# Sigmoids and the softmax division as exponentials of minus a logarithm, w_out by half columns first, GLA's last step one group later

## The reference, cut to what matters

```python
u = rmsnorm(h, norm1_w)
aq, ak, av, gq, gk, gv, g_lr, g_r, gate_a, gate_b = split(u @ w_in)
# attention: window 128, a sink logit per head joins the softmax
p = softmax(concat([s, sink]))[..., :-1]
attn_o = p @ v
# GLA: decayed state per head, read per chunk
log_a = log_sigmoid(g_lr @ gla_gate_w2 + gla_gate_b) / 16
gla_o = rmsnorm(gla(gq, gk, gv, log_a), gla_norm_w) * silu(g_r)
merged = sigmoid(gate_a) * attn_o + sigmoid(gate_b) * gla_o
h = h + merged @ w_out
v2 = rmsnorm(h, norm2_w)
h = h + (silu(v2 @ w_gate) * (v2 @ w_up)) @ w_down
out = rmsnorm(h, final_norm_w)
```

## Time and profile before

| | |
|---|---|
| median of 3 runs | 4039.02 us (4012.56, 4039.02, 4191.1) |
| the profiled execution | 3989.18 us, span of its slowest core 3987.6 us |
| spans of the eight cores | 3979.7 to 3987.6 us, granted clock 0.978 to 0.979 |
| TensorE (PE) | 3767.8 us busy, 94% of the span |
| VectorE (DVE) | 1285.7 us, 32% |
| ScalarE (ACT) | 806.1 us, 20% |
| GpSimd (POOL) | 194.3 us, 5% |
| chain that ended last | PE 91%, DVE 4%, DMA 2%, issue 1%, ACT 1% |

### The profile page before, as it was taken

One profiled execution on the slowest core, in us unless ns is written; L12 is line 12 of the kernel. 1 busy time (PEld: TensorE's weight loads), 2 busy tenths in 40 slices (PEclk: granted clock), 3 DMA queues, 4 the chain that ended last, 5 costly groups with the idle time before them and its releaser, 6 DMA issues.

```text
span 3987.6 us, 46220 instructions; the slowest of 8 cores (3979.7 to 3987.6 us)
## 1 busy us (share of the span) xinstructions
PE 3767.8 (94%) x18016; PEld 1700.6 (43%) x18016; DVE 1285.7 (32%) x2070; ACT 806.1 (20%) x1549; POOL 194.3 (5%) x361
## 2 busy tenths in 40 slices
PE   4899999996899999999999999999869999999998
PEld 1444444442344444444454444444324444444443
DVE  1225555556331110011112464646553111110113
ACT  1223232322221110000012232323313000000002
POOL 0000000000000000000000000000000000000000
PEclk9999999998999999999999999999989999999999
DMA  6234343435365555457863434333256555555553
GB/s 152 45 64 69 64 69 64 69 64 119 67 166 119 111 102 85 71 109 146 161 126 64 69 64 69 64 69 64 43 137 153 106 109 119 119 106 93 134 103 111
DMA packets 81416, 382.75 MB, mean 96 GB/s; under 512 B 9264, under 2 KB 10416, under 8 KB 44592
## 3 DMA queue, kind: packets, MB, share of 16 engines
q0 software_dynamic: 36432, 260.19, 39.2%
q1 hardware_dynamic: 44768, 119.59, 9.2%
HBM read 594.84 MB, written 44.04 MB: 160 GB/s over the span
## 4 chain that ended last, share of the span: by engine, by line
PE 91%; DVE 4%; DMA 2%; issue 1%; ACT 1%; POOL 0%; DVEq 0%; SPq 0%; ACTq 0%; POOLq 0%
PE ps L331 89%; DMA px_231<-xT 1%; DVE a_t_93 L378 1%; PE ps L339 1%; PE ps L619 1%; DMA h_0_96<-x 1%; DVE xnT_102 L375 1%; POOL st L399 0%; DVE xn_100 L375 0%; DVE mT L369 0%; ACT g_Sb L355 0%; DVE xn_101 L375 0%; DVE g_U L375 0%; DVE a_t_94 L364 0%; DVE a_t_93 L364 0%
## 5 line engine op out<-in xcount | busy, mean ns | idle before, releaser
L378 DVE RECIPROCAL a_t_93<-a_t_93 128x512 f32<-128x512 f32 x64 | 214.5, 3352 | 6.6
L355 ACT ACTIVATE sg_212<-ps 128x512 bf16<-128x512 f32 x88 | 52.5, 597 | 541.5 <-PE ps L331 541.5
L355 ACT ACTIVATE sg_213<-ps 128x512 bf16<-128x512 f32 x88 | 52.6, 598 | 527.8 <-PE ps L331 527.8
L331 PE MATMUL ps<-v2T_163,wu_67 128*128 128x512 bf16 x576 | 136.1, 379 | 0.0
L331 PE MATMUL ps<-v2T_108,wu_68 128*128 128x512 bf16 x576 | 136.1, 379 | 0.0
L331 PE MATMUL ps<-v2T_108,wu_65 128*128 128x512 bf16 x576 | 136.1, 379 | 0.0
L331 PE MATMUL ps<-v2T_108,wu_66 128*128 128x512 bf16 x576 | 136.1, 379 | 0.0
L331 PE MATMUL ps<-v2T_163,wu_69 128*128 128x512 bf16 x576 | 136.1, 379 | 0.0
L331 PE MATMUL ps<-v2T_108,wu_69 128*128 128x512 bf16 x576 | 136.1, 379 | 0.0
L331 PE MATMUL ps<-v2T_163,wu_66 128*128 128x512 bf16 x576 | 136.1, 379 | 0.0
L331 PE MATMUL ps<-v2T_163,wu_65 128*128 128x512 bf16 x576 | 136.1, 379 | 0.0
(11 more groups left out here) (1319 smaller groups left out, 6541.1 us busy)
## 6 DMA issues: line engine op xcount, KB each, us to landing
wu_66<-wmix POOLq DMA_DIRECT2D x24, 1024.0 KB, 13.1
wu_67<-wmix POOLq DMA_DIRECT2D x24, 1024.0 KB, 13.5
wu_65<-wmix POOLq DMA_DIRECT2D x23, 1024.0 KB, 14.4
wu_68<-wmix POOLq DMA_DIRECT2D x23, 1024.0 KB, 11.4
wu_69<-wmix POOLq DMA_DIRECT2D x22, 1024.0 KB, 14.1
wu_69<-wffn POOLq DMA_DIRECT2D x18, 1024.0 KB, 13.4
wu_65<-wffn POOLq DMA_DIRECT2D x18, 1024.0 KB, 14.1
wu_66<-wffn POOLq DMA_DIRECT2D x18, 1024.0 KB, 13.6
```

The costliest lines, as they stand in the source:

```text
L331: r = e.matmul(o_, lhsT=l_, rhs=r_, start=s0, stop=s1)
L355: S.op("act", lambda e: e.activation(out=o_, in_=i_, func=func, scale=scale, **kw), outs, ins)
L378: S.op("dve", lambda e: e.reciprocal(out=o_, in_=a), [o_], [a])
```

## The change

Three edits.

- A sigmoid becomes exp(-ln(1 + exp(-x))), three ScalarE instructions (`sigm`) instead of one tanh; VectorE's instruction behind it becomes a plain multiply. The bf16 tiles `ttb` lie over the float tiles `tts`. For `gate_a` only exp(-x) is kept (`ag`), and `a_back` forms (1 + exp(-x)) times the denominator, takes its logarithm and the exponential of minus it on ScalarE, and multiplies `bo` by that: VectorE loses the reciprocal and one multiply, and gains one combined instruction.
- `d_groups` takes tiles 0 to 3 of the first two column blocks, then tiles 4 to 7 of both, then the last two blocks as before. It is stepped once with one step of `a_chain` for twelve groups, instead of eight groups with two steps each (one after the first group). Four of the five weight buffers are held until the twelfth group.
- `g_chain` yields once more before `s3(7)`, and what is left of it runs ahead of `a_chain` in the next head's `g_proj`, in 18 steps over 32 groups instead of 16. For the last head of a chunk the rest of `g_chain` is run out at the end of `a_proj`, as before.

```diff
--- before.py
+++ after.py
@@ -272,6 +272,7 @@
     ])
     assert gend <= rG + 46 * 1024, (gend - rG) / 1024
     tts = [G["tt0"], G["tt1"]]
+    ttb = [place("ttb%d" % i, [128, 512], BF16, S.base[tts[i].name][0]) for i in range(2)]
     e8, _ = seq(rE, [("a_P%d" % i, [128, 512], BF16) for i in range(4)] + [("a_t1", [128, 512], F32),
                                                                           ("a_t2", [128, 512], F32)])
     n2bc = place("n2bc", [128, D], F32, rE)
@@ -453,7 +454,6 @@
     vset(declast[:], 0.0)
     act(sinkc, sinkc, AF.Exp)
     vts(negb, negb, -1.0, None, ALU.mult)
-    vts(gnwc, gnwc, 0.25, None, ALU.mult)
 
 
     sqb = [G["g_la"], G["g_cum"], G["g_eg"], G["g_ei"]]
@@ -530,6 +530,12 @@
         act(G["g_ei"][:], cum[:], AF.Exp, scale=1.0 / 16)
         cl = cum[:, :].rearrange("p (a b) -> p a b", b=128)[:, :, 127]
         act(dec[:, dk, hf * 4:hf * 4 + 4], cl, AF.Exp, scale=-1.0 / 16)
+
+    def sigm(o_, t, p):
+
+        act(t, p, AF.Exp, scale=-1.0)
+        act(t, t, AF.Ln, bias=1.0)
+        act(o_, t, AF.Exp, scale=-1.0)
 
     def g_proj(c, h):
 
@@ -563,8 +569,8 @@
             b = proj_tok(c, units, 0, 512, i)
             t = tts[rot["tt"] % 2]
             rot["tt"] += 1
-            act(t[:], b[:, :], AF.Tanh, scale=0.5)
-            stt(rs[:, i, :], t[:], 1.0, b[:, :], ALU.add, ALU.mult)
+            sigm(t[:], t[:], b[:, :])
+            vtt(rs[:, i, :], t[:], b[:, :], ALU.mult)
             yield
         drop(units)
         units = take(2)
@@ -572,8 +578,9 @@
             b = proj_tok(c, units, 0, 512, i)
             t = tts[rot["tt"] % 2]
             rot["tt"] += 1
-            act(t[:], b[:, :], AF.Tanh, scale=0.5)
-            stt(rs[:, i, :], t[:], 1.0, rs[:, i, :], ALU.add, ALU.mult)
+            tb = ttb[rot["tt"] % 2]
+            sigm(tb[:], t[:], b[:, :])
+            vtt(rs[:, i, :], tb[:], rs[:, i, :], ALU.mult)
             yield
         drop(units)
 
@@ -590,10 +597,7 @@
                 drop(uq)
             for pr in range(4):
                 b = proj_feat(c, ug, pr * 128, hf)
-                t = tts[rot["tt"] % 2]
-                rot["tt"] += 1
-                act(t[:], b[:, :], AF.Tanh, scale=0.5)
-                vts(ag[:, pr, hf * 512:(hf + 1) * 512], t[:], 0.5, 0.5, ALU.mult, ALU.add)
+                act(ag[:, pr, hf * 512:(hf + 1) * 512], b[:, :], AF.Exp, scale=-1.0)
                 yield
         drop(ug)
 
@@ -649,9 +653,11 @@
         def v4(ap):
             return ap.rearrange("p (a b) -> p a b", a=4)
         vtt(v4(t1[:, :]), v4(bd[:, :]), sinkc[:, h * 4:(h + 1) * 4].unsqueeze(2).to_broadcast([128, 4, 128]), ALU.add)
-        recip(t1[:], t1[:])
-        vtt(t2[:], bo[:, :], t1[:], ALU.mult)
-        vtt(v4(t3[:, :]), v4(t2[:, :]), ag[:, :, n * 128:(n + 1) * 128], ALU.mult)
+
+        stt(v4(t1[:, :]), ag[:, :, n * 128:(n + 1) * 128], 1.0, v4(t1[:, :]), ALU.add, ALU.mult)
+        act(t1[:], t1[:], AF.Ln)
+        act(t2[:], t1[:], AF.Exp, scale=-1.0)
+        vtt(t3[:], bo[:, :], t2[:], ALU.mult)
         mo = mT[:, h * 4:(h + 1) * 4, n * 128:(n + 1) * 128]
         vtt(mo, mo, v4(t3[:, :]), ALU.add)
 
@@ -729,6 +735,7 @@
         if c + 1 < NCH:
             vcopy(declast[:, h, :], dec[:, :, NT - 1])
             store(sd[h], U[:, :, :].rearrange("p a b -> p (a b)"), "us", ("sd", h))
+        yield
         s3(NT - 1)
         yield
 
@@ -742,9 +749,6 @@
             while done < want:
                 next(overlay, None)
                 done += 1
-        for _ in overlay:
-            pass
-
     def chain2(a, b):
         yield from a
         yield from b
@@ -768,9 +772,14 @@
     def d_groups(c):
 
         h1 = h1lo + h1hi[c]
-        for g in range(4):
-            units = take(2)
-            for t in range(NT):
+        held = {}
+        half = NT // 2
+        for g, ts in ((0, range(half)), (1, range(half)), (0, range(half, NT)), (1, range(half, NT)),
+                      (2, range(NT)), (3, range(NT))):
+            if g not in held:
+                held[g] = take(2)
+            units = held[g]
+            for t in ts:
                 b = nps()
                 tl = slice(t * 128, (t + 1) * 128)
                 mm([(b[:, :], mT[:, k, tl], wu[units[k // 8]][:, k % 8, :], k == 0, k == 15) for k in range(16)],
@@ -784,7 +793,8 @@
                         norm_turn(c, t - 2)
                     norm_tail(c, t, h1[t])
                 yield
-            drop(units)
+            if ts[-1] == NT - 1:
+                drop(units)
 
     def e_groups(c):
         for j in range(HC // 2):
@@ -960,11 +970,11 @@
                 for _ in g_proj(c, h):
                     pass
             else:
-                weave(g_proj(c, h), prev, 32, 16)
+                weave(g_proj(c, h), prev, 32, 18)
             ov = g_chain(c, h)
             if h < 3:
                 weave(a_proj(c, h), ov, 16, 18)
-                prev = a_chain(c, h, range(NT))
+                prev = chain2(ov, a_chain(c, h, range(NT)))
             else:
                 ap = a_proj(c, h)
                 for i in range(9):
@@ -984,11 +994,9 @@
             r0 = c * TT + t * 128
             load(h1[t][:], x[r0:r0 + 128, :], "hx%d" % t)
         dg = d_groups(c)
-        for i in range(8):
+        for i in range(12):
             next(dg)
             next(ac, None)
-            if i > 0:
-                next(ac, None)
         for _ in ac:
             pass
         load(n2bc[:], n2b, "n2")
```

## The result

| | kernel before | changed kernel |
|---|---|---|
| profiled execution | 3989.18 us | 3890.68 us, 98.5 less |
| span of its slowest core | 3987.6 us | 3889.1 us |
| ratio of timed runs | | 0.963, 95% interval 0.955 to 0.971 |
| the same, timed again in five rounds | | 0.969, 95% interval 0.9625 to 0.975 |

The median of the four runs is 3966.46 us (3889.47 to 4272.02). In some runs of either kernel a pair of cores or a whole die shows a lower granted clock and a longer span, which lifts that median, and the kernel before more often than the changed one, so what follows compares profiled executions without it (their ratio is 0.975), leaves out the first run with the reciprocal (4248.08 us), and in one experiment takes the four cores that kept their clock.

A forecast was written before the change was run, and what follows sets the result against it. TensorE, busy 94% of the span, was taken as the bound, so only its waits and slow matmuls could be won. 32.9 + 44.6 + 6 = 83 us off 3989.2 gives 3906, plus 23 for timed runs 3930; range 3872 to 3985.

The forecast's parts named there:

- GLA's last step: At head changes, two groups of 6.9 us between s2(7) and s3(7) cover TensorE's 4.36 us wait: gain 32.9 us.
- The start of w_out: First groups of w_out: shorter chain and new group order cut mask waits and slow matmuls, 22.3 us a chunk, 44.6 in all.
- the first block's "2.8 us": At w_out's start, TensorE's 8.00 us wait for the first block falls to 2.8 by one group and a 1.8 shorter chain.
- the later blocks' pace: In w_out, mask to mask falls from 11.54 to 9.7 us against 8.5 of TensorE's work, leaving 1.2 wait a block.
- The DMA "stays": At w_out's first block, VectorE's wait until 979.75 on the residual tile's DMA was expected to remain.
- The last head's a_proj: Six waits for bo, 26.3 us, each become 1.0 us shorter: gain 6 us, between 0 and 12.
- "is worth nothing by itself": Whole kernel: with TensorE busy 94% of the span, a shorter VectorE or ScalarE alone gains nothing.
- The 23 us that I added for timed runs: Whole kernel: the lowest timed run lay 23 us above the profiled execution, so 3906 became 3930.
- More is won: Rival, chance 0.22: w_out's blocks keep up and slow matmuls vanish, 62 us there, 107 in all, 3882 + 23 = 3905.
- ScalarE's order: Rival, chance 0.18: logarithms waiting for VectorE hold up ScalarE's queue; w_out gives 22, a_proj nothing, gate groups lose 10: 3967.
- `g_gn_84` is not late behind two groups: Denies a rival, chance 0.04: at head changes g_gn_84 stays late behind two groups, only w_out gains: 50 us, 3962.
- No table load stood around a square: Denies a rival, chance 0.04: each of GLA's 64 squares brings two table loads, 2.57 us; 65 us slower, 4054.

The follow-up runs named there:

- Early loads and halves: Changed kernel with x's residual rows loaded before GLA's last two steps are run out, each row block in two column halves: 3873.41 us profiled, timed ratio 0.971.

## Why the prediction was right, and where it was not

The forecast was 3930 us for timed runs, in a range of 3872 to 3985, and 3906 for the profiled execution, which took 3890.7.

- **GLA's last step: right.** 30.3 us won against 32.9, and 27.8 lost when it is put back. Two groups cover the wait, as the sum had it. The one cheap head change of chunk 1, counted at 3.48 us, won 2.9; the others won 5.3 to 5.7.
- **The start of w_out: right in size, with errors that cancel, which is luck.** The waits left over are 2.23 + 2.83 + 0.21 + 0.51 + 0.38 = 6.2 us in chunk 0 and 1.90 + 4.52 + 0.21 + 0.38 + 0.39 = 7.4 in chunk 1, 6.4 forecast for each; the rest of the gain, 4.6 and 5.4 us of slow matmuls, was forecast as 6.8. One step that failed is the first block's "2.8 us": it counts the chain to the mask only. The third group needs the first group's bank again (the work between takes the rest of the eight), and that bank waits for the residual addition, so x's load holds up TensorE twice, 2.23 us at the bank and 2.83 at the mask. The other is the later blocks' pace: the sum took 1.8 us off 11.54 for the shorter chain alone. In the old order the shorter chain gave 1.0 (10.55 us a block), in the new order with the reciprocal VectorE is the pace at 11.4, and only both together give 9.1 to 9.2, with 0.2 to 0.5 us of wait instead of 1.2.
- **The DMA "stays" only in a sense.** x's first load took 12.9 us where it took 9.8, being issued 8.9 us behind two units of weights instead of 11.9; in chunk 1 15.5 where it took 13.1, issued 5.3 us behind instead of 7.3. Issued ahead of the weights it took 6.3. Early loads and halves won 14.7 us at the two starts and made the last heads' step worth hiding. No wait for a weight unit came: the one issued at 1002.81 landed in 9.7 us, as the sum had it.
- **The last head's a_proj: under-priced.** `bo`'s six waits fell by 6.9 us (6 forecast), and 10.7 were won up to `w_out`. The shorter chain is more than half of that (the reciprocal put back cost 2.6 and 3.3 us there), and the gate's copy has a part (1.0 and 1.4).
- **What was missed: 17 us.** The sum, 3906 for this execution, was 15 too high. One instruction that the change removes and that I did not cost is worth that much, `gate_a`'s affine copy; the three other terms were off by 2.6, 4.4 and -4.7 us and nearly cancel. The copy is 0.43 us long, and I had written that a shorter VectorE "is worth nothing by itself". But it waited for ScalarE with GLA's scalings behind it, and `g_gn_83`'s waits in the earlier trace rows were its trace. The page "TensorE: Matmul & The Clock Gate" (Trainium skill, section "Architectural detail: the array is 16× 32×32, not 1× 128×128") says that VectorE's queue is strict first-in first-out. The rows at 487.58 and 488.54 agree: VectorE was idle for 1.60 us ahead of the copy, and the scalings behind it began 1.30 us after the transposes where 0.50 are enough without it (486.13 to 486.63).
- **The 23 us that I added for timed runs were not there.** The changed kernel's least times, 3888.97 to 3891.44 us, lie within 2 us of its profile.
- **The rivals.** *More is won*, 3882 without the 23 us, came nearer than the forecast's 3906, though not for its reasons: `w_out` won 40.2 of its 62, and what it lacked was the copy. ScalarE's order did not eat the gain: the logarithm waits for VectorE (0.68 us at 953.80), yet no new wait stands in the gate groups and `bo`'s waits fell as forecast. `g_gn_84` is not late behind two groups. No table load stood around a square: 6 loads in all. And 70 loads cost nothing measurable, so that rival's price was wrong as well as its condition (its 4054 also leaves out the 23 us that the others carry). The page "ScalarE: Activation LUTs" (Trainium skill, section "What ACT_TABLE_LOAD costs") gives 2.66 us for a switch; by it 64 more would be an estimated 170 us of ScalarE. The rows show 1.28 us for each load, and no difference in the kernel's time.

## What to carry to other kernels

Price an instruction by what stands behind it in its queue while it waits for another engine, not by its length: 64 copies of 0.43 us, on an engine busy 32% of the span, cost 14 to 21 us of the kernel's time. Where a ring through three engines paces a stretch, a shorter chain alone (4.5 and 4.9 us here) or more work beside it alone (16.0 and 13.9) does not give the whole (23); measure the four corners before dividing the gain between them. And after each gain look which transfer is waited for now: hiding the last step's wait was worth nothing until x came earlier, and 4 us a chunk after that.

## What was not expected of the hardware

A table load was followed by its activation 1.30 us after its start, and began 0.02 us after the activation before it had ended (tanh, then a block's logarithm and exponential, in the kernel with tanh):

```profile
407.56 1.28 ACT L356 ACT_TABLE_LOAD   x1 [2.27 <-DVE a_t L376]
408.86 1.35 ACT L356 ACTIVATE a_t<-a_t 128x512 f32<-128x512 f32 x2
410.23 1.28 ACT L356 ACT_TABLE_LOAD   x1
411.53 0.60 ACT L356 ACTIVATE tt<-ps 128x512 f32<-128x512 f32 x1
```
